# Gate and up weights side by side in one transfer, the last down chunk of a layer in three, in a two-layer transformer kernel

## What is computed

```python
for l in range(DEPTH):                      # 2 layers
    h = _rms_norm(x, norm_mix[l])
    z = h @ w_in[l]                         # 1024 x 3000, in six column chunks
    ...                                     # three attentions -> ya, yb, yc
    x = x + mix @ w_out[l]                  # 1024 x 1024, in two column halves
    x = x + _hier_moe(_rms_norm(x, norm_ffn[l]), ...)
return _rms_norm(x, norm_final)

def expert_block(args):                     # inside _hier_moe, for 32 experts a layer
    xb, e = args
    h = jax.nn.silu(xb @ w_gate[e]) * (xb @ w_up[e])     # 1024 x 512 each
    return h @ w_down[e]                                 # 512 x 1024
```

## Time and profile before

| | |
|---|---|
| median of 3 runs | 1188.37 us (1188.06 to 1188.47) |
| profiled execution, first to last instruction | 1185.7 us |
| PE busy | 921.0 us (78%) |
| DMA, mean over the span | 378 GB/s |
| stage of experts, layer 0 | 162 to 592 us |
| stage of experts, layer 1 | 747 to 1177 us |

### The profile page before, as it was taken

The page is one execution under the profiler, slowest core; times in us unless marked ns, Lnnn a source line. Parts: engine busy times, 40 slices in busy tenths (PEclk is TensorE's granted clock), DMA queues, the critical chain, the costliest instruction groups (busy, mean ns, idle before and its releaser), DMA issues.

```text
span 1185.7 us, 23487 instructions
## 1 busy us (share of the span) xinstructions
PE 921.0 (78%) x10312; PEld 605.4 (51%) x10317; DVE 333.8 (28%) x974; ACT 195.9 (17%) x529; POOL 18.4 (2%) x37
## 2 busy tenths in 40 slices
PE   9999999766676676766799999997585847566765
PEld 5876566444444343434478766665253525334532
DVE  3555652211111111111147465521111111111112
ACT  2244331010100010101022442211010101000102
POOL 1000000000000000000010001000000000000000
PEclk9999999987888789888999999999787978798888
DMA  8976499999999999999998156999999999999994
GB/s 304 389 299 236 194 366 428 428 423 429 424 429 423 428 425 426 426 427 425 403 388 324 46 226 269 378 425 426 427 424 428 426 425 427 425 427 425 425 428 206
DMA packets 60504, 447.80 MB, mean 378 GB/s; under 512 B 10832, under 2 KB 16368, under 8 KB 33264
## 3 DMA queue, kind: packets, MB, share of 16 engines
q1 hardware_dynamic: 57664, 443.49, 90.7%
q10 hardware_dynamic: 2736, 2.76, 0.7%
HBM read 442.57 MB, written 3.67 MB: 376 GB/s over the span
## 4 chain that ended last, share of the span: by engine, by line
DMA 60%; PE 35%; issue 1%; DVE 1%; SPq 1%; ACT 1%; POOL 0%; POOLq 0%; ACTq 0%; DVEq 0%
DMA ring<-in_w_up 41%; DMA arena<-in_w_up 11%; PE pv L1818 9%; PE pj L1439 8%; DMA arena<-in_w_down 8%; PE pj L1445 2%; PE pj L1545 2%; PE pj L1676 2%; PE pj L1651 1%; PE pj L1685 1%; PE tr L1840 1%; PE lg L1469 1%; SPq L593 1%; PE tr L1479 1%; PE pj L1850 1%
## 5 line engine op out<-in xcount | busy, mean ns | idle before, releaser
L1818 PE MATMUL pv<-ring,xT 128*32 128x256 f32 x3136 | 293.0, 454 | 145.8 <-DMA ring<-in_w_up 92.7
L1818 PEld LDWEIGHTS pv<-ring,xT 128*32 128x32 f32 x3136 | 147.4, 126 | 241.3 <-issue 191.9
L1284 DVE TENSOR_SCALAR arena<-arena 128x128 f32<-128x128 f32 x64 | 14.5, 227 | 678.7 <-ACT arena L860 678.4
L1818 PE MATMUL pv<-arena,xT 128*32 128x256 f32 x640 | 89.2, 436 | 28.7 <-DMA ring<-in_w_up 28.7
L675 ACT ACTIVATE arena<-pv 128x256 f32<-128x256 f32 x64 | 24.6, 384 | 525.8 <-PE pv L1818 525.8
L1439 PE MATMUL pj<-xT,ring 128*128 128x256 f32 x448 | 100.3, 381 | 0.0
L1840 PE MATMUL tr<-ring,arena 128*32 128x256 f32 x1376 | 83.0, 379 | 15.1 <-issue 15.1
L1439 PEld LDWEIGHTS pj<-xT,ring 128*128 128x128 f32 x448 | 84.1, 190 | 13.3 <-issue 1.2
L1850 PE MATMUL pj<-arena 32*128 32x256 f32 x512 | 72.5, 399 | 8.1 <-ACT arena L675 8.1
L1850 PE MATMUL lg<-arena 32*128 32x256 f32 x512 | 72.5, 400 | 0.0
L1818 PEld LDWEIGHTS pv<-arena,xT 128*32 128x32 f32 x640 | 46.1, 121 | 47.5 <-issue 39.6
(11 more groups left out here) (244 smaller groups left out, 950.7 us busy)
## 6 DMA issues: line engine op xcount, KB each, us to landing
ring<-in_w_gate SPq DMA_DIRECT2D x46, 2048.0 KB, 44.6
ring<-in_w_up SPq DMA_DIRECT2D x46, 2048.0 KB, 38.9
ring<-in_w_down SPq DMA_DIRECT2D x42, 2048.0 KB, 42.9
arena<-in_w_down SPq DMA_DIRECT2D x14, 2048.0 KB, 45.1
arena<-in_w_gate SPq DMA_DIRECT2D x12, 2048.0 KB, 44.8
ring<-in_w_in SPq DMA_DIRECT2D x10, 2048.0 KB, 21.2
arena<-in_w_up SPq DMA_DIRECT2D x8, 2048.0 KB, 39.3
ring<-in_w_out SPq DMA_DIRECT2D x4, 2048.0 KB, 21.3
```

Source lines behind the costliest of these rows:

```text
L1818: ins = mm(gu_ps[i * CAP:(i + 1) * CAP, :], xg[:, j, c:c + CAP], w, start=(j == 0), stop=(j == KD - 1), tile_position=(0, i * CAP), skip_g ...
```

## The change

Gate and up of an expert are laid side by side in HBM and in SBUF: a partition has eight steps, each 512 gate and then 512 up values, in one run of 32 KB, loaded by one transfer of 4 MB into one of four double places (three pairs of ring slots, one in `arena`). Down weights have three places of their own (ring slots 7 and 6, and `x` with `bias`, which are now one tile `xb`, so that this place too is filled by one transfer). Expert `e` uses place `e % 4` for gate and up and `e % 3` for down; the table of homes is gone. `w_in` and `w_out` are laid out ahead too, so that a partition's share of a chunk is one run (16 KB; 14 KB for the first). The last down chunk of a layer comes in three transfers (steps 0 and 1, step 2, step 3), and PE waits for each ahead of its steps.

```diff
+GU_PLACES, D_PLACES = 4, 3
+LAST_PIECES = ((0, 2), (2, 3), (3, 4))
-        win_v = w_in.rearrange("l (p j) n -> l p j n", j=KD)
-        wout_v = w_out.rearrange("l (k p) n -> l p k n", k=KD)
-        gate_v = w_gate.rearrange("l e (p j) d -> (l e) p j d", j=KD)
-        up_v = w_up.rearrange("l e (p j) d -> (l e) p j d", j=KD)
+        gu_v = gate_up_d.rearrange("e p (j n) -> e p j n", j=KD)
+        wout_v = w_out_d.rearrange("l h p (k n) -> l h p k n", k=KD)
...
+            def first_experts(l):
...
+                again = gu[REFILLED]
+                sp.wait_ge(steps_used, at(l, 2, 1))
+                sp.dma_start(gu_place[0][:, 0:2], again[:, 0:2]).then_inc(refill_in, 16)
+                sp.wait_ge(steps_used, at(l, 2, 2))
+                sp.dma_start(gu_place[0][:, 2:4], again[:, 2:4]).then_inc(refill_in, 16)
+                sp.wait_ge(gu_used[0], at(l, GU_FILLS, 1))
+                sp.dma_start(gu_place[0][:, 4:], again[:, 4:]).then_inc(gu_full[0], 16)
...
+                    for kind, e in loads_of(m):
+                        if kind == "gu" and e > REFILLED:
+                            i = e % GU_PLACES
+                            sp.wait_ge(gu_used[i], at(l, GU_FILLS, gu_uses(e)))
+                            sp.dma_start(gu_place[i], gu_v[l * N_EXPERTS + e]).then_inc(gu_full[i], 16)
+                        elif kind == "d" and e >= SPLIT:
+                            i = e % D_PLACES
+                            sp.wait_ge(d_used[i], at(l, D_FILLS[i], d_uses(e)))
+                            rows_of = down_v[l * N_EXPERTS + e]
+                            if e == N_EXPERTS - 1:
+                                for n, (a, b) in enumerate(LAST_PIECES):
+                                    sp.dma_start(d_place[i][:, a:b], rows_of[:, a:b]).then_inc(last_in[n], 16)
...
-                def down(rows_of, b):
+                def down(rows_of, b, in_pieces=False):
 
                     for k in range(KE):
+                        for n, (first, _) in enumerate(LAST_PIECES):
+                            if in_pieces and k == first:
+                                pe.wait_ge(last_in[n], 16 * (l + 1))
```

More of the change, by code:

```diff
@@ L126, in bucket_one_hot @@
     return (np.arange(REL_BUCKETS)[:, None] == bucket[None, :]).astype(np.float32)
[L129 to L149, removed]
@@ L152, in loaded_in_order @@
[L152 to L182, removed]
@@ L185, with loads_of @@
[L185 to L196, removed]
+def loads_of(m):
+    order = [("gu", 0)]
+    for e in range(1, BODY - 1):
+        order += [("gu", e), ("d", e - 1)]
+    late = [("gu", BODY - 1), ("d", BODY - 2)] if m == ROUNDS - 1 else [("d", BODY - 2), ("gu", BODY - 1)]
+    return [(kind, m * BODY + e) for kind, e in order + late + [("d", BODY - 1)]]
@@ new lines, with gu_uses, d_uses, gu_loads @@
+GU_PLACES, D_PLACES = 4, 3
+GU_LOADS = {1: 2, 2: 2}
+D_LOADS = {1: 2, 2: 2}
+SPLIT = GU_PLACES - 1
+REFILLED = GU_PLACES
+LAST_PIECES = ((0, 2), (2, 3), (3, 4))
+GU_FILLS = N_EXPERTS // GU_PLACES
+D_FILLS = [len(range(i, N_EXPERTS, D_PLACES)) for i in range(D_PLACES)]
+def gu_uses(e):
+    return sum(n % GU_PLACES == e % GU_PLACES for n in range(e))
+def d_uses(e):
+    return sum(n % D_PLACES == e % D_PLACES for n in range(e))
+def gu_loads(layer, e):
+    def upto(last):
+        return sum(GU_LOADS.get(n, 1) for n in range(last) if n % GU_PLACES == e % GU_PLACES)
+    return 16 * at(layer, upto(N_EXPERTS), upto(e + 1))
@@ L199, in at, with d_loads, upto @@
+def d_loads(layer, e):
+    def upto(last):
+        return sum(D_LOADS.get(n, 1) for n in range(last) if n < N_EXPERTS - 1 and n % D_PLACES == e % D_PLACES)
+    return 16 * at(layer, upto(N_EXPERTS), upto(e + 1))
 def at(layer, per_layer, n):
@@ L327, in trunk @@
         junk = rows[:, 1, 0:512]
-        extra = (arena[:, ARENA - SLOT:], arena[:, ARENA - 2 * SLOT:ARENA - SLOT],
-                 (x.rearrange("p t f -> p (t f)"), bias[:, 0:8, :].rearrange("p h k -> p (h k)")))
+        late_place = arena[:, ARENA - 2 * SLOT:]
+        flat_ring = ring.rearrange("p s n -> p (s n)")
+        gu_place = [flat_ring[:, 2 * i * SLOT:2 * (i + 1) * SLOT].rearrange("p (j n) -> p j n", j=KD) for i in range(3)]
+        gu_place.append(late_place.rearrange("p (j n) -> p j n", j=KD))
+        d_place = [flat.rearrange("p (k n) -> p k n", k=KE) for flat in (ring[:, 7, :], ring[:, 6, :], xb[:, 0:SLOT])]
         taken[0] = 0
@@ L435, in chunk, with win_v @@
             return ring[:, s, 0:KD * n].rearrange("p (j n) -> p j n", j=KD)
[L437 to L453, removed]
+        def win_v(l, i):
+            a, b = WIN_CHUNKS[i]
+            at_ = KD * sum(q - p for p, q in WIN_CHUNKS[:i])
+            return w_in_d[l][:, at_:at_ + KD * (b - a)].rearrange("p (j n) -> p j n", j=KD)
         def nk(t):
@@ L1675, in out_upper @@
                     for k in range(KD // 2, KD):
-                        mm(pj[:, half], mixT_up[:, t, k - KD // 2, :], weights(6 + half)[:, k, :], start=(k == KD // 2), stop=False)
+                        mm(pj[:, half], mixT_up[:, t, k - KD // 2, :], chunk(6 + half, 512)[:, k, :], start=(k == KD // 2), stop=False)
                 def out_lower(t, half):
@@ L1809, in gather, with gate_up @@
                     return last
-                def gate_up(gate, up, c, other_half=0, signal=False):
+                def gate_up(both, c, other_half=0, signal=False):
                     for j in range(KD):
@@ L1938, in _ @@
                                 pe.wait_ge(over_full[0], i * 16 + 16)
-                                pe.wait_ge(over_full[1], i * 16 + 16)
-                                gate, up = (chunk(slot_of(l, c), 512) for c in range(2))
-                                gate_up([gate[:, j] for j in range(KD)], [up[:, j] for j in range(KD)], 0).then_inc(o_gu, 1)
+                                gate_up(gu_place[0], 0).then_inc(o_gu, 1)
                                 pe.wait_ge(o_gu_read, i + 1)
```

249 lines of the change are left out of this document (117 added, 132 removed).

## The result

| | before | after |
|---|---|---|
| median, same chip, 4 runs each | 1188.21 us (1187.81 to 1188.47) | 1195.12 us (1194.47 to 1196.44) |
| ratio, 95% interval | | 1.0061 (1.0047 to 1.0075) |
| span of the profiled execution | 1185.7 us | 1194.6 us |
| attention, layer 0 (to PE's products(0)) | 161.9 us | 170.7 us |
| experts, layer 0 (to PE's first step of layer 1) | 430.7 us | 430.3 us |

The change made the kernel slower by 6.9 us, where 7.6 us of gain were forecast. The table, read from the starts of PE's products(0) and of the first step of layer 1, says where to look: 8.8 us are lost before the first expert, and the two stages of experts, from which 9.2 us were to come, gave nothing. The table is of one execution each, and the profiled one of the changed kernel is the slowest of its four (1196.44 us): its span grew by 8.9 us where the medians differ by 6.9.

A forecast was written before the change was run, and what follows sets the result against it. Attention was taken to go at PE's pace and the experts at DMA's; -5.6 - 2.4 - 1.2 + 1.6 = -7.6 us took 1188.4 to 1180.8 us, range 1173.5 to 1187, chance 0.50.

The forecast's parts named there:

- Term 1: Expert stream: longer runs save fixed packet parts, 4.5 us for 54 experts plus 1.1 for the two-halves place: 5.6 us gained.
- Rival A: Expert stream: a 32 KB run is still two packets, so 4.5 us are missing: 1185.3 us; chance 0.20.
- rival D: Expert stream: 32 KB runs are slower by themselves, reads lying farther apart in HBM; at 3%, 16 us, 1197 us; chance 0.11.
- Rival C: Expert stream: merging also removes losses at transfers' ends, 5.5 us more gained, 1175.3 us; chance 0.07.
- Term 2: Refill behind expert 0: three longer-run transfers instead of six lose less DMA time, 1.2 us a layer, 2.4 gained.
- Term 3: Layer's end: last down chunk in pieces removes PE's waits of 0.66 and 0.52 us, 1.2 us gained.
- Other edits cost nothing: Semaphores, overflow code and places in fixed turn were put at no cost, nine queued transfers covering the places.
- Term 4: Layer 0 attention: long w_in packets delay ACT's store of bias lines, landing 42.7 us; cost 1.6 us, bounds 0 and 4.7.
- stays so: Layer 0 attention: PE, 1.6 us late behind the lines, keeps that delay, as it runs without a gap from there.
- rival B: Layer 0 attention loses more: lines land at 45.8 us, PE is 4.7 us late, 1183.9 us; chance 0.12.
- An ACT wait longer than 5 us: Sign named against the forecast, for attention losing more by the late bias lines.

The follow-up runs named there:

- e6: e5 with gate and up laid out in two halves, so the same single transfer has 16 KB packets instead of 32 KB: 1184.09 us.
- e4: Changed kernel with w_in and w_out in 2 KB runs again and expert 29's down weights loaded ahead of expert 30's gate and up: 1178.84 us.
- e5: Changed kernel, long runs kept, expert 29's down weights before expert 30's gate and up, SP's wait for lines ahead of layer 0's fourth w_in chunk: 1178.88 us.
- e7: e5 with the last down chunk of a layer in one transfer again: 1180.96 us.
- e1: Changed kernel with w_in and w_out read again in 2 KB runs from their original layout: 1186.14 us.
- e2: Changed kernel with expert 29's down weights loaded ahead of expert 30's gate and up in each layer's last round: 1187.85 us.
- e11: e2 with 28 products of zeros on PE in its gap at the start of layer 0: 1185.93 us.
- e3: Kernel before with only the long-run layout of w_in chunks and w_out halves: 1197.10 us.
- e8: e2 with w_in laid out in runs of 4 KB: 1180.01 us.
- e9: Changed kernel, loads unchanged, but PE and ACT take expert 30's products ahead of expert 29's down step in the last round: 1190.32 us.

## Why the prediction was wrong

**Term 1** (-5.6 us, longer runs) was right. The part for the 54 experts was 4.5 us by 10.3 ns a packet; e6 measured 5.2. Rival A (32 KB cut in two) and rival D (a slower stream) fall with 429 GB/s. Rival C (5.5 us more than packets) falls too: e4, without the two faults, gains 9.8 us where terms 1 to 3 gave 9.2. Rival D's price had been borrowed from the Trainium skill's rule on large row pitches ("DMA: Bandwidth & Descriptors", "Latency and other measured facts"), whose figures are of copies between HBM tensors and not of loads, as I had put it; runs of 32 KB that follow each other without a gap show no such loss here.

**Term 2** (-2.4 us, the refill) was not run alone, but e4's trace has the stretches of the earlier trace rows, at the same distance from products(0):

```profile
164.22:170.72 6.50, 5.89 (x110) 3.34 (x106) 5.76 (x21) 0.66 (x2) 0.00 (x0) 1.00 1.00 405
746.63:753.13 6.50, 5.89 (x108) 3.34 (x104) 5.66 (x21) 0.66 (x2) 0.00 (x0) 1.00 0.97 401
```

At 433 GB/s, 405 for 318 and 401 for 319 are 1.3 and 1.2 us less lost in the two layers, 2.5 together. The stretch of 165 to 200 us says the same, 426 GB/s in e5 and 410 before, 1.3 us in layer 0. After the parts of e6 and e7, 2.5 us of e4's 9.8 are left for this and for term 1's smaller part (1.1 us). The size fits; the smaller part can't be told from the scatter.

**Term 3** (-1.2 us, pieces) was right of a kernel whose tail is as before, as e5 and e7 show. In the changed kernel PE's last product starts straight behind its own work, and the pieces gain nothing.

**"Other edits cost nothing" is the first step that failed:** a term that I had put at nothing. I priced the fixed places as a question of whether SP issues in time, and nine transfers in the queue answered that. I did not hold the new order of the loads against PE's order in the last round, although both stand in the kernel: the old `chunks_of` left expert 29's down weights ahead of expert 30's gate and up, the new `loads_of` puts them behind. Price: 7.3 us (e1 less e4), against 9.2 expected from terms 1 to 3. Note what hid it: the 10.4 us of idle PE are no measure. The loss is how much later PE's chain ends than the last byte allows.

**Term 4 (+1.6 us, the lines) is the second step that failed**; the mechanism was right and the size was not. It measured 9.0 us (e2 less e4), past its high bound of 4.7. By its parts:
- The lines landed at 47.5, not 42.7. I let the third chunk start at 19 us since SP had fewer runs to issue. Its first packets moved at 21 and the engines were full at 22, as before; SP's own issues ran from 13.92 to 18.3 us, so it was not SP's issuing that held the chunk back until 21, and what did stays open. And I let the lines start 1.6 us after their issue (22.94 to 24.5). Their first packet was at 25.8 us in the changed kernel and at 26.7 in the one before, 3.9 and 3.7 us after the issue: that trace had it, and I took the delay from a general allowance. (Of SP's transfers on an idle queue it showed yet another one, 0.95 us where I had put 1.5.) The row said when the store was issued and when it had landed; I needed its first packet.
- The landing 4.8 us later than forecast moved PE from 1.6 to 6.3 us late: this step of the working held.
- The clock had no place in the sum at all. I wrote that PE "stays so"; the engine that stood idle 7.1 us came back at a clock of 0.63, and the stretch behind took 2.4 us more, of which e11 gave back 1.9 by the medians.

The rule in the Trainium skill that I weighed there ("DMA: Bandwidth & Descriptors", "Queues, rings and completion order") says that an engine drains a packet of several descriptors before it changes the queue. I read it as making the term zero; that needs several line runs to share a turn while the long runs of `w_in` do not, which the page does not say. The traces show single turns instead: at all three sizes packets of the profile, one run each, pass one for one, 1047 to 1008, 830 to 832 and 235 to 233, and e3 with 1197.1 us shows what that costs.

So rival B had the right mechanism, 0.12 of the chance and half the price, and no rival had the tail. "An ACT wait longer than 5 us" was named as the sign against the forecast; it came with 10.09 us.

## What to carry to other kernels

When loads are reordered or put into fixed places, write the new order of loads beside the order in which the engine takes them, at the ends of loops most of all: a stream that is bound by bytes hides every mismatch but the last. Long runs belong in a stream that is alone; where a small transfer on another queue is waited for, first let it pass, then issue the long ones (here one wait moved ahead by three chunks kept both gains, 1178.9 us). And when a change makes TensorE wait on a path that it bounds, add what it loses behind the wait.

## What the runs showed of the hardware

- Two queues that share a DMA engine take turns by packets, whatever their size: 1.5 KB against 2, 4 and 16 KB gave ratios of 1.04, 1.00 and 1.01 (27 us on, in the kernel before, e8 and the changed kernel). The 1.5 MB store took 14.1, 19 and 25.5 us from issue to landing.
- Its first packet moved 3.7 and 3.9 us after ACT's issue (kernel before, changed kernel).
- A run of 32 KB stays one packet: 1221 ns on the mean of 200 to 560 us in e5, two of 16 KB in e6 2 x 618. The fixed part of a packet is 12 to 15 ns by an estimate from these and from the 5.2 us of e6.
- TensorE's granted clock after idling: 10.4 us without work, then 0.50 over 3.8 us (changed kernel, layer 0); 7.1 us, then 0.63 over 6.8 us (the same, start); 3.1 us, then 0.57 over 8 us (e9); 0.45 us, then 1.00 over 6.8 us (e8). Products of zeros in the gap kept it at 1.00 both times.
